# Rotary halves of fifteen blocks exchanged by SBUF transfers instead of a matrix product

## The reference, cut to what matters

```python
def apply_rope(x, cos, sin):
    half = x.shape[-1] // 2
    x1, x2 = x[..., :half], x[..., half:]
    return jnp.concatenate([x1 * c - x2 * s, x2 * c + x1 * s], axis=-1)

# diff_attention
q = apply_rope(q.reshape(B, S, 2 * H, d), cos, sin).reshape(B, S, H, 2, d)
k = apply_rope(k.reshape(B, S, 2 * H, d), cos, sin).reshape(B, S, H, 2, d)
s = einsum('bqhcd,bkhcd->bhcqk', q_blk, k) * scale     # causal
p = softmax(s);  a = p[:, :, 0] - lam * p[:, :, 1];  o = a @ v
```

## Time and profile before

| | |
|---|---|
| median of 3 runs | 1135.86 us (1135.41 to 1136.42) |
| profiled execution | 1135.31 us |
| its span, first to last instruction | 1134.0 us |
| granted TensorE clock, mean | 0.999 |
| busy: TensorE, VectorE, ScalarE, GpSimd | 1118.3, 821.5, 637.4, 56.6 us |
| packets of DMA queue q1 (SyncE's), q10 (ScalarE's) | 225.59 MB, 4.45 MB |

### The profile page before, as it was taken

How to read it: one execution, slowest core, us unless ns; L and a number is a source line. 1 busy time by engine, 2 the same in 40 slices (tenths; PEclk the granted TensorE clock), 3 DMA queues, 4 the chain that set the end, 5 groups by cost and what they waited for, 6 DMA issues and landing times.

```text
span 1134.0 us, 16844 instructions
## 1 busy us (share of the span) xinstructions
PE 1118.3 (99%) x6542; PEld 979.6 (86%) x6542; DVE 821.5 (72%) x1416; ACT 637.4 (56%) x1203; POOL 56.6 (5%) x68
## 2 busy tenths in 40 slices
PE   8999999999999999999999999999999999999997
PEld 6998989799987888888899988888889988888886
DVE  6998788798666766676777867766667866766665
ACT  6664354856746655555765546555456654555553
POOL 2200000000001000000012300000000100000000
PEclk9999999999999999999999999999999999999999
DMA  9989999684232666668453336555554434655530
GB/s 385 420 314 383 298 389 261 233 337 159 98 112 75 231 219 208 238 223 191 147 202 112 112 112 223 186 186 188 188 182 162 173 107 150 213 190 191 193 128 37
DMA packets 36992, 231.10 MB, mean 204 GB/s; under 512 B 6825, under 2 KB 8241, under 8 KB 9522
## 3 DMA queue, kind: packets, MB, share of 16 engines
q1 hardware_dynamic: 31536, 225.59, 56.4%
q10 hardware_dynamic: 5378, 4.45, 1.3%
HBM read 228.95 MB, written 1.07 MB: 203 GB/s over the span
## 4 chain that ended last, share of the span: by engine, by line
PE 87%; DVE 5%; ACT 4%; DMA 2%; issue 1%; POOL 1%; ACTq 0%; DVEq 0%; POOLq 0%
PE ps L1718 43%; PE pacc L1718 42%; ACT whi L1998 1%; DVE wlo L2270 1%; DMA raw<-in_stream 1%; ACT arena L2105 1%; DMA cl<-in_cols 1%; POOL st L2600 1%; ACT wk L2208 0%; PE ps L1857 0%; PE ps L1928 0%; DVE wlo L2280 0%; ACT arena L1998 0%; DVE st L2495 0%; DVE h L2386 0%
## 5 line engine op out<-in xcount | busy, mean ns | idle before, releaser
L2270 DVE TENSOR_TENSOR wlo<-raw,whi 128x1024 fp32r<-128x1024 f32 x346 | 414.9, 1223 | 115.3 <-ACT whi L1998 114.8
L1718 PE MATMUL ps<-both,whi 128*128 128x256 f32 (+2 forms) x1728 | 460.6, 339 | 1.9 <-ACT both L1998 1.0
L1998 ACT ACTIVATE whi<-raw 128x1024 fp32r<-128x1024 f32 x346 | 360.4, 1056 | 98.4 <-PE ps L1718 44.1
L1718 PE MATMUL ps<-both,wlo 128*128 128x256 f32 x1264 | 354.6, 281 | 0.0
L1718 PEld LDWEIGHTS ps<-both,whi 128*128 128x128 f32 (+1 forms) x1728 | 296.7, 189 | 42.3 <-issue 3.7
L1718 PEld LDWEIGHTS ps<-both,wlo 128*128 128x128 f32 x1264 | 238.8, 189 | 2.9
L1718 PE MATMUL pacc<-whi,both 128*128 128x512 f32 (+2 forms) x352 | 106.5, 383 | 1.2 <-ACT both L2121 0.6
L1998 ACT ACTIVATE sg<-ps 128x256 f32<-128x256 f32 (+1 forms) x98 | 37.3, 380 | 100.3 <-PE ps L1718 100.1
L2290 DVE SCALAR_TENSOR_TENSOR raw<-raw,silu_c 128x1024 f32<-128x1024 f32 x72 | 89.8, 1255 | 3.6 <-DMA raw<-in_stream 3.6
L1718 PE MATMUL pacc<-whi,mhi 128*128 128x512 f32 x228 | 90.7, 398 | 0.0
L1718 PE MATMUL pacc<-whi,mlo 128*128 128x512 f32 x228 | 89.4, 392 | 0.0
(11 more groups left out here) (280 smaller groups left out, 1470.3 us busy)
## 6 DMA issues: line engine op xcount, KB each, us to landing
raw<-in_stream SPq DMA_DIRECT2D x213, 1024.0 KB, 5.0
gates<-gate_rows ACTq DMA_DIRECT2D x3, 512.0 KB, 7.4
h<-in_x SPq DMA_DIRECT2D x2, 512.0 KB, 4.4
cst<-in_const ACTq DMA_DIRECT2D x1, 1024.0 KB, 4.7
arena<-bias_rows ACTq DMA_DIRECT2D x1, 1024.0 KB, 28.6
arena<-in_final_g SPq DMA_DIRECT2D x1, 512.0 KB, 5.8
out<-tmp SPq DMA_DIRECT2D x2, 256.0 KB, 2.0
out<-tmp ACTq DMA_DIRECT2D x2, 256.0 KB, 2.3
```

The costliest lines, as they stand in the source:

```text
L1718: return e.matmul(o, a, b, start=start, stop=stop)
L1998: return e.activation(o, a, ACT.Copy, **how)
L2270: return e.tensor_tensor(o, a, hi.bitcast(F32), ALU.subtract)
```

## The change

For the first fifteen of the sixteen blocks `roped` is replaced by `swapped`. ScalarE copies the bank into one of three slots in the arena. SyncE then issues four SBUF to SBUF transfers of 32 rows of 1 KB each (32 KB a transfer), which write the rows exchanged by 32 into a second part of the slot. GpSimd multiplies the copy by the cosine as before. VectorE multiplies the exchanged rows by a sine table that now carries the sign, and adds. The bank is given back after the copy. The matrix `rot` of the remaining rotations (the last key block of this stage and those of the third layer) loses its sign for the same reason.

The end of a rotation (`rope_close`) is no more a part that nudges advance. It is emitted at the end of the next turn, behind that turn's `feed`. `rest[0]` is 1 in this loop. The chunk loads of the stage are kept as `owed` by `feed` and issued by ScalarE in the next turn, behind its copy of the block.

```diff
@@ -242,13 +242,26 @@
             return [(P * k, P, COLS["kv_in_g"] + k) for k in range(8)]
         return []
 
+    owed, loader = [], ["sp"]
+
     def load_chunk():
+        if loader[0] == "act":
+            owed.append(0)
+        else:
+            load_next()
+
+    def load_owed():
+        while owed:
+            owed.pop()
+            load_next()
+
+    def load_next():
         n = pos["chunk"]
         if 2 * n >= len(stream):
             return
         pos["chunk"] += 1
         free = [t for u in (2 * (n - NR), 2 * (n - NR) + 1) for t in raw_free.get(u, [])]
-        add("load", chunk=n, free=latest(*free))
+        add("load", chunk=n, free=latest(*free), lane=loader[0])
 
     def feed(until=None, limit=100):
         while not hold and limit and pos["unit"] < (until or len(stream)):
@@ -1271,6 +1284,22 @@
         ys.give(yb, t)
         yield t
 
+    slots, swaps = Places([Place(n) for n in range(3)]), Counter()
+
+    def swapped(dst, split, b, tk, s, by):
+        slot = slots.take()
+        n, (at, t_tables) = slot.at, by
+        x, y = tick("rpc"), tick("rpz")
+        swaps[n] += 64
+        add("rope_swap", b=b.at, full=tk, s=s, n=n, free=slot.free, at=at, tables=t_tables, copied=x)
+        banks.give(b, x)
+        yield
+        sine = tick("rps")
+        add("rope_close", n=n, cosine=y, swapped=(f"swap{n}", swaps[n]), sine=sine, at=at, dst=dst, split=split)
+        t = tick("rpd", 2 if split else 1)
+        slots.give(slot, t)
+        yield t
+
     turns, by_r = [], []
 
     def during_v():
@@ -1344,17 +1373,29 @@
         t_q[at], born[at] = next(rope), side.now
         yield
 
+    pending, rest[0], loader[0] = [], 1, "act"
     for hh in range(8):
         for g in (0, 8):
             if hh == 7:
                 banks.retire(fix[2:4] if g else fix[0:2])
             b = banks.take()
             tk = block(b, 0, unit(("qk", g + hh)), n1, side.nudge)
-            rope = roped(("kT", hh) if g else ("qT", hh), not g, b, tk, 1.0 if g else 0.125, by_r)
+            last = g and hh == 7
+            rope = (roped if last else swapped)(("kT", hh) if g else ("qT", hh), not g, b, tk, 1.0 if g else 0.125, by_r)
             next(rope)
+            load_owed()
             side.nudge()
             feed()
-            side.soon(rope_end(g + hh, rope))
+            if pending:
+                at, was = pending.pop()
+                t_q[at], born[at] = next(was), side.now
+            if last:
+                side.soon(rope_end(g + hh, rope))
+            else:
+                pending.append((g + hh, rope))
+    load_owed()
+    loader[0] = "sp"
+    rest[0] = 2
     while banks.leaving:
         side.step(False)
     cross = Whole([(n1, ("cl", COLS["mlp_g"]), None, list)])
@@ -1621,6 +1662,10 @@
         self.ul = self.view(4096, 2, T)
         self.fg = self.arena[:, 6144:7168]
 
+    def swap_slot(self, n):
+        x, y = self.view(4096, 8, T), self.view(11776, 3, T)
+        return x[:, n, :], x[:, 3 + n, :], y[:, n, :]
+
     def view(self, at, n, width):
         return self.arena[:, at:at + n * width].rearrange("p (n r) -> p n r", n=n)
 
@@ -1692,10 +1737,16 @@
     e.dma_start(m.h[:, 0, :], d["x"][0:P, :]).then_inc(S["x0"], 16)
     e.dma_start(m.h[:, 1, :], d["x"][P:T, :]).then_inc(S["x1"], 16)
     for st in steps:
-        if st.kind == "load":
+        if st.kind == "load" and st.lane == "sp":
             q.room(st.free)
             n = st.chunk % NR
             e.dma_start(m.raw[:, n, :], d["stream"][st.chunk]).then_inc(S[f"raw{n}"], 16)
+        elif st.kind == "rope_swap":
+            q.wait_ge(*st.copied)
+            x, s, _ = m.swap_slot(st.n)
+            for a in range(0, P, 32):
+                c = a ^ 32
+                e.dma_start(s[a:a + 32, :], x[c:c + 32, :]).then_inc(S[f"swap{st.n}"], 16)
         elif st.kind == "lambda_load":
             q.wait_ge(*st.after)
             e.dma_start(m.lrow, bass.AP(tensor=d["lam"].tensor, offset=d["lam"].offset, ap=[[0, P], [1, 256]])).then_inc(S["lamrow"], 16)
@@ -2012,6 +2063,10 @@
                 t.then_inc(S["hi"], 1)
             else:
                 copy(hi, raw).then_inc(S["hi"], 1)
+        elif kind == "load" and st.lane == "act":
+            q.room(st.free)
+            n = st.chunk % NR
+            e.dma_start(m.raw[:, n, :], d["stream"][st.chunk]).then_inc(S[f"raw{n}"], 16)
         elif kind == "opening":
             for f in range(2):
                 q.wait_ge("acc", f + 1)
@@ -2235,6 +2290,10 @@
             q.wait_ge(*st.full)
             q.room(st.x_free)
             copy(m.sg[:, st.x, :], m.bank(st.b)[:, 0:T], scale=st.s).then_inc(S["rpx"], 1)
+        elif kind == "rope_swap":
+            q.wait_ge(*st.full)
+            q.room(st.free)
+            copy(m.swap_slot(st.n)[0], m.bank(st.b)[:, 0:T], scale=st.s).then_inc(S["rpc"], 1)
         elif kind == "lambda":
             q.wait_ge("lam", 2)
             e.activation(m.stat(st.le, 2), m.stat(st.ls, 2), ACT.Exp).then_inc(S["lexp"], 1)
@@ -2531,6 +2590,19 @@
                     e.tensor_tensor(to[r, 2 * n + c, :], x[r, :], y[r, :], ALU.add).then_inc(S["rpd"], 1)
             else:
                 e.tensor_tensor(o, o, y, ALU.add).then_inc(S["rpd"], 1)
+        elif kind == "rope_close":
+            what, h = st.dst
+            _, s, y = m.swap_slot(st.n)
+            q.wait_ge(*st.swapped)
+            q.wait_ge(*st.cosine)
+            o = s if st.split else m.kT[:, h, :]
+            e.tensor_tensor(o, s, m.rope_table(st.at, "sin"), ALU.mult).then_inc(S["rps"], 1)
+            q.wait_ge(*st.sine)
+            if st.split:
+                for c, r in enumerate(LOHI):
+                    e.tensor_tensor(m.qT[r, 2 * h + c, :], s[r, :], y[r, :], ALU.add).then_inc(S["rpd"], 1)
+            else:
+                e.tensor_tensor(o, o, y, ALU.add).then_inc(S["rpd"], 1)
         elif kind == "lambda":
             q.wait_ge("lamrow", 16)
             l4, lp = m.lrow.rearrange("p (a d) -> p a d", a=4), m.arena[:, 10496:10624].rearrange("p (a d) -> p a d", a=2)
@@ -2620,6 +2692,11 @@
             if st.tables:
                 q.wait_ge(*st.tables)
             e.tensor_tensor(m.hm[:, st.y, :], m.sg[:, st.x, :], m.rope_table(st.at, "cos"), ALU.mult).then_inc(S["rpy"], 1)
+        elif kind == "rope_swap":
+            q.wait_ge(*st.copied)
+            q.wait_ge(*st.tables)
+            x, _, y = m.swap_slot(st.n)
+            e.tensor_tensor(y, x, m.rope_table(st.at, "cos"), ALU.mult).then_inc(S["rpz"], 1)
 
 
 def build(nc, stream, x, c_row, cols, const, rel, lam, final_g, out):
@@ -2648,10 +2725,7 @@
     put("ident", np.eye(P))
     r = np.zeros((P, P))
     for m in range(P):
-        if m % 64 < 32:
-            r[m + 32, m] = -1.0
-        else:
-            r[m - 32, m] = 1.0
+        r[m + 32 if m % 64 < 32 else m - 32, m] = 1.0
     put("rot", r)
     put("flip", np.eye(P)[::-1])
     put("tri", (i[:, None] >= i[None, :]).astype(np.float32))
@@ -2661,7 +2735,7 @@
     inv = (np.float32(10000.0) ** (-np.arange(0, 64, 2, dtype=np.float32) / np.float32(64))).astype(np.float32)
     ang = (np.arange(T, dtype=np.float32)[:, None] * inv[None, :]).astype(np.float32)
     put("cos", np.cos(ang).astype(np.float32).T[i % 32])
-    put("sin", np.sin(ang).astype(np.float32).T[i % 32])
+    put("sin", np.sin(ang).astype(np.float32).T[i % 32] * np.where(i % 64 < 32, -1.0, 1.0)[:, None].astype(np.float32))
     t = np.arange(T)
     m = np.where(t[None, :] > t[:, None], MASKED, 0.0)
     put("topk", m.reshape(2, P, T).transpose(1, 0, 2).reshape(P, 2 * T))
```

More of the change, by code:

```diff
@@ L1540 @@
     "xsq", "xg", "xnew", "xrow", "xz", "xzd", "xah", "xhi", "xlo", "phi", "plo", "fin", "wa", "wb",
-    "ixc", "ixt", "mod", "g8", "masks", "tabc",
+    "rpc", "rpz", "swap0", "swap1", "swap2", "ixc", "ixt", "mod", "g8", "masks", "tabc",
     "lows", "sums", "sg", "hm", "hhi", "hlo", "rsilu", "rgate",
```

## The result

The changed kernel takes 1152.51 us (median of 4 runs, 1151.90 to 1153.62) against 1135.63 us of the kernel before on the same chip: ratio 1.0143, interval [1.0129, 1.0156], which is 16.9 us slower. The direction was forecast, the size was not: 1142 with a range to 1149.

What follows compares the result with a forecast made beforehand. TensorE is busy 99% of the span, but in the stage VectorE's turn is slower. New TensorE waits of 13.30 us against 6.74 gained give +6.56 on 1135.31: 1142 us, range 1137 to 1149.

Steps and rivals of the forecast that it cites:

- The order: Key close behind a split and directly ahead of its head's maxima on VectorE; TensorE stands 1.91 or 2.37 us a head.
- The sum: Six heads in the stage: 13.30 us of new TensorE waits against 6.74 gained, so +6.56 us; chance 0.63.
- What is removed: Fifteen rot products off TensorE at 0.43 us each, plus a 0.29 us wait for ScalarE's copy: 6.74 us gained.
- the rival of the exchange that is hidden: Closes done before TensorE reaches the logits, so the whole 6.74 us is kept: 1128.6; chance 0.08.
- What stays the same: Work on VectorE, ScalarE and GpSimd unchanged; sine from SBUF at 0.42 us, possibly 0.1 more a block.
- The transfers: SyncE's exchanges, 3.3 to 6.2 us from copy to data, taken as 0 cost; 3.5 us a key block at the high end.
- the exchanges come late: Key exchange over 5.2 us from the copy makes VectorE stand; at 8.7 us, +21 more, 1163; chance 0.07.
- The loads on ScalarE: Load issued behind the next query block's copy: only 0.33 us in ScalarE's chain per two blocks.
- A TensorE busy time that is some 7 us less: Sign expected in the profile after: TensorE's busy time some 7 us less, in a longer span.

Runs made afterwards that it cites:

- no exchange, fill, no cosine: Changed kernel without its sixty transfers, with filling products ahead of the masks, and without GpSimd's fifteen cosine products: 1144.50 us, ratio 1.0067, stage +7.43 us.
- rest3: Changed kernel with rest[0] 3 instead of 1, so part A of a head stands one block later: 1139.60 us, ratio 1.0034.
- the sine from PSUM: Kernel before without the fifteen rot products, VectorE's sine multiplication reading the block's PSUM bank, halves not exchanged: 1133.44 us, ratio 0.9978.
- the candidate: Changed kernel with rest[0] 3, loads issued by SyncE, and the query blocks' sine product on GpSimd instead of VectorE: 1142.05 us, ratio 1.0051.
- the old order: As a run: changed kernel with the close back in the middle of the next block and rest[0] 2; transfers and loads as changed: 1154.00 us, ratio 1.0150.

## Why the prediction was right in direction and wrong in size

The stage's 16.50 us come apart by differences of the kernels above:

| part | from | us |
|---|---|---|
| order of steps, less the removed products | no exchange, fill, no cosine | 7.43 |
| VectorE's mix beside GpSimd's cosine | 9.32 - 7.43 | 1.89 |
| late exchange at head 0, and lower clock | 16.50 - 9.32 | 7.18 |

The last row is 3.9 us for the exchange alone (16.50 - 12.60) and 4.2 for the clock alone (16.50 - 12.27), less 0.95 that falls away with either of the two. Each of these differences can be off by the 1 us or so by which stages and medians disagree. The forecast held the first row only. What failed is that its sum put three terms at nothing: the neighbours of GpSimd's cosine (1.89 us measured), the exchange and the load beside it (3.9 us), and the clock behind the waits (4.2 us).

**"The order": right.** The step list, the key addition as what ends each wait, and VectorE's wait for its own head's logits (1.08 us where 0.97 was priced) are all in the trace. With rest3, whose edit alters only this, 13.2 us go, the lower clock among them. (The head whose logits stand at 618.24 in the earlier trace rows is head 3 counted from 0; the prediction calls it head 4, which touches no number.)

**"The sum" for the order: 6.56 forecast, 7.43 measured.** The period is 11.10 us without disturbance where 10.97 was worked out. Here the mechanism was right and the size nearly so.

**"What is removed", 6.74 us gained: borne out as TensorE's work, misleading as a gain.** Used in the sum against VectorE's turn it was sound, since the periods were compared whole. But for the rival of the exchange that is hidden it gave 1128.6, and the most that the removal gives in the old order is 2.25 us (the sine from PSUM). The rival was priced by TensorE while VectorE's 10.00 us were there to be read the earlier trace rows.

**"What stays the same", the sine at 0.42 or 0.1 more: the operation's own time was right here, the neighbours were not looked at.** In the changed kernel the sine keeps 0.41 to 0.42; what got longer is the mix, 1.14 for 0.75, because GpSimd's cosine moved beside it. In the order of before, with the rot products left out, it is the sine itself, 0.95. 1.89 us were left out.

**"The transfers", taken as 0: failed at head 0.** Four issues were priced by a load's 0.33 us and take 0.59. From the end of the copy of block 1 (583.79) to its data (592.06) it was 8.3 us, outside the 3.3 to 6.2 taken and inside the 8.7 kept as an upper end; the room was 5.3. The rival "the exchanges come late" put this on all six heads; in the changed kernel it came at the first only, where two blocks' exchanges follow each other and the first load is beside them.

**"The loads on ScalarE", only 0.33 us: failed.** Their issue costs what was said (0.35), but with the loads moved back to SyncE, 3.0 to 3.8 us were gone and the exchange of the first head was in time. By which path the other queue does this (the DMA engines' time, or the order in which they take the two queues) was not separated, and the candidate had a late exchange with the loads on SyncE.

**The lower clock was not thought of.** The row says 1.00, and the prediction kept it although it forecast TensorE to stand six times. It costs 4.2 us, or 3.3 without the exchange (12.60 - 9.32).

**Waits by head**: forecast 1.91, 1.91, then 2.37 four times; measured 5.05, 1.60, 2.37, 2.55, 1.98, 2.54. Apart from the first they come to 11.04 against 11.39, which looks better than it is. The forecast was the length of a turn less TensorE's 8.60, and by that measure the turn of 11.40 at full clock costs 2.80 where 2.37 was forecast; idle time shows 0.25 less of it, and after 5.05, 2.55 and 2.54 the lower clock fills part of the next turn with work. Two errors of opposite sign met. "A TensorE busy time that is some 7 us less" failed: it rose by 0.7. In the stage the lower clock gave back 4.2 us (112.23 against 108.00 with rest3), and part of the rest is the ends of products that stand in front of waits.

## What to carry to other kernels

Before you price an instruction taken off the busiest engine, measure the period of the next one over the same loop: here TensorE had 9.46 us and VectorE 10.00 a head, and 6.5 us of products taken out were worth 2.25 at best. Then ask where the finishing step of the new path stands in its engine's queue; one step directly ahead of the instruction that waits for its result turned a slack of 2.35 us into a wait of some 2.4 us in each turn. Price a small transfer with its own issues and with whatever load shares the DMA engines at that moment, and a forecast of waits on TensorE with a lower clock behind them.

## What the hardware showed that was not expected

- SyncE takes 0.59 us to issue an SBUF to SBUF transfer of 32 rows of 1 KB, and 0.33 us for a load of 1 MB that stands alone (all 23 loads of the kernel before from 560 to 720 us). With the loads on SyncE, a load directly behind an exchange took 0.58 us (at 589.72), so the kind of transfer alone does not decide it. A 32 KB transfer landed in 1.8 to 5.4 us.
- Waits of about 2 to 2.5 us were followed by logits at a lower clock in some cases and not in others: in the changed kernel behind 5.05, 2.55 and 2.54 us but not behind 2.37 and 1.98; without the exchange behind a wait of 1.93 at head 0 (2.58 us for the group), but with rest3 not behind 2.14 (1.55 us). In the old order a wait of 1.08 was followed by a group of 2.90, where another wait of 2.57 had ended 2.6 us before. The wait's own length does not decide it. What does stays open; no run here separates it.
- Of two instructions that get in each other's way only one became longer, and it was the one that started second. In the kernel before without rot, VectorE's low part started at 624.87 and kept its 1.22 us; GpSimd's cosine started at 625.01 and took 1.66 instead of 0.74; the sine behind it started at 626.00 and took 0.95 instead of 0.42. In the changed kernel the cosine started at 619.42 and kept its 0.74 us, and the mix, from 619.56, took 1.14 instead of 0.75.
